# Earlier first loads in the attention head, and two low halves and an affine step moved in the pooling stage, of a two-block transformer kernel

## The reference, cut to what matters

```python
# layer 0, the head of the kernel
sh1, sc1, g1, sh2, sc2, g2 = split(silu(c) @ w_mod[0] + b_mod[0])    # w_mod: 1024 x 6144
hx = x * (1 + sc1) + sh1           # latent tokens
hc = ctx * (1 + csc1) + csh1       # 256 context tokens
q = rope(hx @ w_qkv[:, :1024]); k, v from hx and hc with the other columns
...
# layer 1, the pooling stage, between the first feed-forward and the second
x  = layer_norm(ALPHA * x + g2 * (hidden @ ffn_w_out[0]))
hx = x * (1 + sc1) + sh1
pooled = window means of hx (windows 2, 4, 8, 16) - hx
x  = layer_norm(ALPHA * x + g1 * ((pooled @ w_pool) * pool_scale))
h  = (x * (1 + sc2) + sh2) @ ffn_w_in[1] ...
```

## Time and profile before

| | |
|---|---|
| median of three runs | 1114.23 us (1114.17 to 1116.12) |
| profiled execution | 1114.73 us |
| its span, first to last instruction | 1113.0 us |
| PE busy | 1099.3 us, 99% of the span |
| DVE busy | 776.3 us, 70% |
| ACT busy | 587.0 us, 53% |
| chain of work that ended last | PE 92%, DVE 3%, DMA 3%, ACT 1% |

### The profile page before, as it was taken

How to read it: one execution, slowest core, us unless ns; L and a number is a source line. 1 busy time by engine, 2 the same in 40 slices (tenths; PEclk the granted TensorE clock), 3 DMA queues, 4 the chain that set the end, 5 groups by cost and what they waited for, 6 DMA issues and landing times.

```text
span 1113.0 us, 14486 instructions
## 1 busy us (share of the span) xinstructions
PE 1099.3 (99%) x5851; PEld 910.0 (82%) x5851; DVE 776.3 (70%) x1007; ACT 587.0 (53%) x821; POOL 61.4 (6%) x118
## 2 busy tenths in 40 slices
PE   8999999999999999999999999999999999999998
PEld 4688766899998887888887878878888888888886
DVE  2596588889889797877745865455566677774454
ACT  3742376563454347555534767556754466563342
POOL 0011200002121001000000000000000000000000
PEclk9999999999999999999999999999999999999999
DMA  9987740679999946667567788786524455555541
GB/s 363 403 309 249 243 163 1 208 255 349 379 383 332 350 146 232 224 211 269 183 199 126 223 177 190 155 180 134 177 76 152 152 196 203 207 189 189 189 161 38
DMA packets 111986, 238.31 MB, mean 214 GB/s; under 512 B 5712, under 2 KB 51920, under 8 KB 110640
## 3 DMA queue, kind: packets, MB, share of 16 engines
q1 hardware_dynamic: 97280, 185.42, 53.2%
q0 software_dynamic: 14352, 51.72, 13.1%
q10 hardware_dynamic: 288, 0.26, 0.1%
HBM read 236.29 MB, written 1.07 MB: 213 GB/s over the span
## 4 chain that ended last, share of the span: by engine, by line
PE 92%; DVE 3%; DMA 3%; ACT 1%; issue 0%; SPq 0%; ACTq 0%
PE ps L2068 19%; PE ps L2069 19%; PE ps L2070 19%; PE ps L2136 10%; PE ps L2138 5%; PE ps L2105 4%; PE ps L2104 4%; PE ps L2103 4%; PE ps L2253 2%; DMA raw<-in_attn_w_qkv 2%; PE ps L2388 1%; PE ps L2356 1%; DMA raw<-in_qkv_first 1%; DVE wL L1213 1%; PE ps L2277 0%; PE ps L2621 0%
## 5 line engine op out<-in xcount | busy, mean ns | idle before, releaser
L1213 DVE TENSOR_TENSOR wL<-raw,wH 128x1024 fp32r<-128x1024 f32 x326 | 394.7, 1222 | 211.3 <-ACT wH L638 208.9
L638 ACT ACTIVATE wH<-raw 128x1024 fp32r<-128x1024 f32 x326 | 340.3, 1058 | 300.4 <-PE ps L2070 196.1
L2068 PE MATMUL ps<-wH,aHL 128*128 128x512 f32 x576 | 229.3, 398 | 2.4 <-DVE aHL L1616 0.9
L2069 PE MATMUL ps<-wL,aHL 128*128 128x512 f32 (+1 forms) x592 | 229.0, 387 | 0.0
L2070 PE MATMUL ps<-wH,aHL 128*128 128x512 f32 x576 | 224.8, 390 | 0.0
L2136 PE MATMUL ps<-aHL,wH 128*128 128x512 f32 x480 | 168.8, 397 | 0.0
L2068 PEld LDWEIGHTS ps<-wH,aHL 128*128 128x128 f32 x576 | 108.1, 188 | 35.1 <-issue 7.1
L2138 PE MATMUL ps<-aHL,wL 128*128 128x256 f32 x480 | 134.1, 279 | 0.0
L2069 PEld LDWEIGHTS ps<-wL,aHL 128*128 128x128 f32 x592 | 111.3, 188 | 20.8
L2070 PEld LDWEIGHTS ps<-wH,aHL 128*128 128x128 f32 x576 | 108.1, 188 | 23.4
L2136 PEld LDWEIGHTS ps<-aHL,wH 128*128 128x128 f32 x480 | 90.1, 188 | 21.7
(11 more groups left out here) (330 smaller groups left out, 1491.7 us busy)
## 6 DMA issues: line engine op xcount, KB each, us to landing
raw<-in_ffn_w_in SPq DMA_DIRECT2D x88, 512.0 KB
modraw<-in_mod_rows POOLq DMA_DIRECT2D x80, 512.0 KB, 6.6
raw<-in_w_in SPq DMA_DIRECT2D x32, 1024.0 KB
raw<-in_ffn_w_out SPq DMA_DIRECT2D x22, 1024.0 KB
raw<-in_w_up SPq DMA_DIRECT2D x16, 1024.0 KB
raw<-in_w_down SPq DMA_DIRECT2D x16, 1024.0 KB
mod<-in_mod_first SPq DMA_DIRECT2D x8, 1024.0 KB, 16.8
raw<-in_attn_w_qkv SPq DMA_DIRECT2D x8, 1024.0 KB
```

The costliest lines, as they stand in the source:

```text
L638: nc.scalar.activation(wHigh(n), raw[:, (n // 2) % RAW, (n % 2) * 1024:(n % 2) * 1024 + 1024], ACT.Copy).then_inc(w_hi, 1)
L1213: V.tensor_tensor(wL[:, n % WL, :], raw[:, (n // 2) % RAW, (n % 2) * 1024:(n % 2) * 1024 + 1024], wHigh(n).bitcast(fp32), ALU.subtract).th ...
L2068: T.matmul(outp, xh, h, start=first, stop=False, skip_group_check=part_of)
L2069: T.matmul(outp, xh, l, start=False, stop=False, skip_group_check=part_of)
```

## The change

In the head: each half of `mod0` and the first half of each query weight get a semaphore of their own. ACT's `adv` of an even sub below 8 waits for the first half only. The load of `cb` moves behind sub 11, the loads of `cst`'s second part and `x` behind sub 15, and ACT's `silu` of `cb` from group 2 to the place behind `adv(16)`. PE does `mod_mm(0)` without waiting for `cst`, has fewer filler calls (5 to 3, 4 to 3, and 1 to 0), and takes `mod_mm(s + 1)` one part earlier. ACT and DVE take `adv(6)` ahead of `mod_copy(3)` and `mod_put(3)`. The tiles `cols` and `vcol` are widened from 113 to 128 and from 80 to 96 columns.

In the pooling stage: `adv(first + 2)` and `adv(first + 3)` on DVE move into `residual(0)` and `residual(1)`, behind the first half of each. `affine(1)` moves ahead of `adv(first + 4)`.

```diff
-        cols = sb(ctx, "cols", [P, 113])
+        cols = sb(ctx, "cols", [P, P])
-        vcol = sb(sA, "vcol", [P, len(VECS) * KT])
+        vcol = sb(sA, "vcol", [P, 96])
-        mod0_in = [sem(f"mod0_in{i}") for i in range(NMOD0)]
+        mod0_in = [sem(f"mod0_in{i}") for i in range(2 * NMOD0)]
+        q_first = [sem(f"q_first{i}") for i in range(4)]
 # SP
             for m in range(NMOD0):
                 for h in range(2):
-                    ... .then_inc(mod0_in[m], 16)
+                    ... .then_inc(mod0_in[2 * m + h], 16)
-                for c in range(2):
-                    sp.dma_start(raw[:, m, c * D:(c + 1) * D], a["qkv_first"][:, m, c, :]).then_inc(w_raw[m], 16)
-                if m == 1:
-                    sp.dma_start(cb[:, :], a["c"].to_broadcast([P, D])).then_inc(cb_in, 16)
+                sp.dma_start(raw[:, m, 0:D], a["qkv_first"][:, m, 0, :]).then_inc(q_first[m], 16)
+                sp.dma_start(raw[:, m, D:2 * D], a["qkv_first"][:, m, 1, :]).then_inc(w_raw[m], 32)
             for c in range(2, 6):
                 chunk(SUBS["qkv"] + 4 * c, a["attn_w_qkv"][0], c * CW)
                 if c == 2:
+                    sp.dma_start(cb[:, :], a["c"].to_broadcast([P, D])).then_inc(cb_in, 16)
+                elif c == 3:
                     sp.dma_start(cst[:, C_DIST:C_END], ...)
                     sp.dma_start(x[:, :, :], ...)
 # ACT
-                if n % 2 == 0:
+                if n < 8 and n % 2 == 0:
+                    act.wait_ge(q_first[n // 2], 16)
+                elif n < 8 or n % 2 == 0:
                     act.wait_ge(w_raw[(n // 2) % RAW], 32 * (n // WL + 1))
             for c in range(NMOD0):
+                if c == 3:
+                    adv(2 * c)
                 if c:
                     act.wait_ge(mod_sel, c)
                 mod_copy(c)
-                adv(2 * c)
+                if c < 3:
+                    adv(2 * c)
                 act.wait_ge(mod_out, c + 1)
                 hi_x(c, *mc(c))
                 adv(2 * c + 1)
-                if c == 2:
-                    act.wait_ge(cb_in, 16)
-                    nc.scalar.activation(cb[:, :], cb[:, :], ACT.Silu).then_inc(cb_ready, 1)
             for c in range(2, 6):
                 for j in range(3):
                     adv(n + 4 * c + WS + j)
+                    if (c, j) == (2, 0):
+                        act.wait_ge(cb_in, 16)
+                        nc.scalar.activation(cb[:, :], cb[:, :], ACT.Silu).then_inc(cb_ready, 1)
                     if (c, j) == (2, 1):
                         heads_out(0)
 # DVE, head
             for c in range(NMOD0):
+                if c == 3:
+                    adv(2 * c)
                 mod_put(c)
-                adv(2 * c)
+                if c < 3:
+                    adv(2 * c)
 # DVE, ln_pool
                 def residual(t):
                     for b in range(2):
                         ...
                         V.bn_stats(...).then_inc(dve_self, 1)
                         links[0] += 1
+                        if b == 0:
+                            adv(first + 2 + t)
                 for j in range(2):
                     low(j)
-                adv(first + 2)
                 for j in range(2, 4):
                     low(j)
                 ...
                 hat(0, halves[1], ln_hat)
-                adv(first + 3)
+                dve.wait_ge(pool_h, TT + 1)
+                affine(1)
                 adv(first + 4)
                 low_x3(0, 0, 0)
                 adv(first + 5)
                 low_x3(0, 0, 1)
-                dve.wait_ge(pool_h, TT + 1)
-                affine(1)
                 scaled(1)
 # PE
-                pe.wait_ge(mod0_in[c], 32)
                 for h in range(2):
+                    pe.wait_ge(mod0_in[2 * c + h], 16)
-            zero_mm(5, 4)
-            pe.wait_ge(cst_in, 16)
+            zero_mm(3, 4)
             pe.wait_ge(cT_ready, 2)
             mod_mm(0)
+            pe.wait_ge(cst_in, 16)
             mod_select(0)
-            zero_mm(4, 5)
+            zero_mm(3, 5)
             for s in (1, 2):
                 q_mm(0, s)
+                mod_mm(s + 1)
                 q_mm(1, s, range(1))
-                mod_mm(s + 1)
-                q_mm(1, s, range(1, 2))
                 mod_select(s + 1)
-                q_mm(1, s, range(2, 4))
-                if s == 1:
-                    zero_mm(1, 5)
+                q_mm(1, s, range(1, 4))
```

More of the change, by code:

```diff
@@ L467, in _ @@
                 for h in range(2):
-                    sp.dma_start(mod0[:, 2 * m + h, :], a["mod_first"][:, m, h, :]).then_inc(mod0_in[m], 16)
+                    sp.dma_start(mod0[:, 2 * m + h, :], a["mod_first"][:, m, h, :]).then_inc(mod0_in[2 * m + h], 16)
                 sp.dma_start(xT[:, 2 * m:2 * m + 2, :], a["x_cols"][:, 2 * m:2 * m + 2, :]).then_inc(x_in[m], 16)
-                for c in range(2):
-                    sp.dma_start(raw[:, m, c * D:(c + 1) * D], a["qkv_first"][:, m, c, :]).then_inc(w_raw[m], 16)
-                if m == 1:
-                    sp.dma_start(cb[:, :], a["c"].to_broadcast([P, D])).then_inc(cb_in, 16)
+                sp.dma_start(raw[:, m, 0:D], a["qkv_first"][:, m, 0, :]).then_inc(q_first[m], 16)
+                sp.dma_start(raw[:, m, D:2 * D], a["qkv_first"][:, m, 1, :]).then_inc(w_raw[m], 32)
             sp.dma_start(ctxT, a["ctx_cols"]).then_inc(ctx_in, 16)
@@ L690, in mod_copy @@
                 nc.scalar.activation(modrow[:, :], ps[:, 6, :], ACT.Copy).then_inc(mod_row, 1)
-            act.dma_start(cols[:, :], a["cols"]).then_inc(cols_in, 16)
+            act.dma_start(cols[:, 0:113], a["cols"]).then_inc(cols_in, 16)
             act.dma_start(cst[:, 0:C_DIST], cst_d[:, 0:C_DIST]).then_inc(cst_in, 16)
```

## The result

The changed kernel takes **1106.71 us** (median of four runs, 1105.58 to 1107.98) where the kernel before took 1114.90 beside it (1114.17 to 1116.12). The ratio is 0.9926, with a 95% interval of 0.9909 to 0.9943: 8.2 us, or 0.7%, faster. The forecast was 1114.3, and its range ended at 1111.6.

What follows compares the result with a forecast made beforehand. PE, busy 99% of the span, was taken as the bound, with one load setting the head and DVE's queue the pooling stage. Head +1.0 and pooling -0.9 on 1114.23 gave 1114.3 us, range 1111.6 to 1116.8.

Steps and rivals of the forecast that it cites:

- item 7: Head, widened tiles: the shift of tiles behind them gets no price; bound 0 to 1.0 us of landing time.
- two events that the prediction named as proof against it: Head: the landing of subs 16 and 17 moves by more than a microsecond, or the clock falls.
- item 4: Head, ACT: adv(6) waits for its load, mod_copy(3) cannot start before 38.6, holding mod_select(3) for about 1 us.
- Item 1: Head, first loads with own signals: PE's first query product starts 1.2 to 1.3 us sooner, near 15.2.
- item 5: Head: the load of subs 16 and 17 lands at 65.4 as before, so nothing is left of PE's 1.5 us lead.
- Item 6: Head, ACT: silu of cb between adv(16) and adv(17) costs +1.0 us; heads(1) moves to 69.05, PE's wait becomes 3.1.
- rival B: Head: the clock falls in the 3.1 us wait before heads(1), costing 1.8 us, giving 1116.1; chance 0.27.
- The estimate of 1.6 us in the prediction: Head loads: by the skill's 256-byte descriptor rule, landing would come 1.6 us earlier; not counted in the sum.
- The steps behind: Pooling stage: pooled(1) and its chain come 1.0 us sooner, and PE wins 1.6 us from later waits.
- the one in front: Pooling stage: residual(1) ends about 0.8 us late, so PE waits +0.7 us for hm before the second window products.
- Rival D: Pooling stage: the 0.7 us delay stays since the waits behind are ACT's, giving 1115.9; chance 0.15.
- C: Head: the load of subs 16 and 17 is not the bound and lands sooner, giving 1110.8 to 1111.8; chance 0.15.

Runs made afterwards that it cites:

- a1: The kernel before with only the two tiles cols and vcol widened; 1106.59 us, ratio 0.9923.
- a3: The head's part of the change alone on the kernel before, narrow tiles, pooling stage as before; 1116.16 us, ratio 1.0018.
- a2: The changed kernel with the narrow tiles, so the whole change without the widening; 1115.16 us, ratio 1.0003.
- a4: The kernel before with the pooling stage's part of the change alone, narrow tiles; 1113.79 us, ratio 0.9988.
- g1: The changed kernel with the silu of cb moved ahead of adv(16) on ACT; 1105.90 us, ratio 0.9921.
- c1: The changed kernel with every tile 32 bytes later, weights too, so all at 160; 1108.87 us, ratio 0.9941.
- c2: The changed kernel with a 128-byte gap behind lrw: tiles behind it at 256, weights and aHL at 128; 1114.64 us, ratio 0.9990.
- c3: The changed kernel with a 256-byte gap behind lrw: tiles behind it at 384, weights and aHL at 128; 1108.48 us, ratio 0.9942.
- b2: The changed kernel with gaps that move wH from 128 to 160 and, unintended, hH to 256; 1114.84 us, ratio 0.9996.
- b3: The changed kernel with gaps that move aHL from 128 to 160 and, unintended, hH and uH to 256; 1118.07 us, ratio 1.0023.

## Why the prediction was wrong

**The step that failed is item 7 of the head: "Instructions get no price, as no row shows one that depends on this."** A row did. The page and the groups of before hold `aHL` at 390 ns and `hH` and `uH` at 395, in products of one shape, one line and one weight tile. I had worked out that the widening moves the tiles behind it, and then looked only at loads for an effect. The grouped rows of PE would have asked the question: what do `hH` and `uH` have in common that `aHL` has not? The size follows from counts, as an estimate. 528 matmuls with `hH` or `hL` at 6.9 ns less per step and 384 with `uH` or `uL` at 6.6 give 3.6 + 2.5 us. 96 with `cH` or `cL` and 96 with `oa`, taken at 6.6 too, give 1.3. That is 7.4 us where item 7 had nothing. a1 measured 8.6 (7.1 to 9.9), so 1.2 us (-0.3 to 2.5) of it is not accounted for; the row of line 2136 under a1 shows that profiled executions differ by more than that for another, unknown reason.

Neither of the two events that the prediction named as proof against it came up where it looked for them. The load kept its time, and in the changed kernel's profile the granted clock is 1.00 from 66 to 80 us. Both watch the head, and nothing in the list of signs watched the pace of a matmul.

**Head, items 1 to 6.** The path was right and the figures near. `adv(6)` stands ahead of `mod_copy(3)` and waits for its load; timeline of ACT in the changed kernel:

```profile
38.31 1.06 ACT L641 ACTIVATE wH<-raw 128x1024 fp32r<-128x1024 f32 x1 [1.75 <-DMA raw<-in_qkv_first]
40.23 0.60 ACT L693 ACTIVATE modrow<-ps 128x512 f32<-128x512 f32 x1 [0.86 <-PE ps L2286]
```

The adv was forecast at 37.6 to 38.6 and ran from 38.31 to 39.37. But the copy behind it then waited 0.86 us for PE, so it was not `adv(6)` that held it in this execution, in which PE was late for the reason below. In a3, where PE was not late, the copy follows `adv(6)` at once, at 38.78 (38.6 forecast), as item 4 has it; timeline of ACT:

```profile
38.78 0.58 ACT L693 ACTIVATE modrow<-ps 128x512 f32<-128x512 f32 x1
```

Item 1 forecast the first query product at 15.2. In a3 it started at 15.26, but in the changed kernel's profiled execution at 16.98, later than before. Timelines of PE, a3 and then the changed kernel, and the changed kernel's windows from 5 to 17 us:

```profile
11.80 2.82 PE L2303 MATMUL ps<-g1b 128*128 128x512 f32 x6
15.26 0.47 PE L2077 MATMUL ps<-wH,aHL 128*128 128x512 f32 x1 [0.63 <-DVE aHL L1321]
```

```profile
12.50 5.47 PE L2303 MATMUL ps<-g1b 128*128 128x512 f32 x6
16.98 1.42 PE L2077 MATMUL ps<-wH,aHL 128*128 128x512 f32 x1
```
```profile
5.00:12.00 7.00, 3.98 (x25) 1.35 (x23) 0.00 (x0) 0.91 (x3) 0.00 (x0) 0.97 1.01 375
12.00:17.00 5.00, 5.00 (x10) 2.42 (x10) 2.74 (x6) 3.82 (x6) 0.00 (x0) 0.50 1.01 425
```

The six fillers took 5.47 us for 2.82, at a granted clock of 0.50 (the 1.2 GHz level) over the whole window; in the 7 us ahead of it PE had been busy for 3.98. This cost nothing at the end, as item 5 has it: PE's work ahead of `heads(1)` is slack, and the wait became 1.5 us (3.1 forecast). In a3, with the full clock there, it is 3.09, as forecast. Item 6 had `heads(1)` at 69.05: 68.88 in the changed kernel, 68.87 in a3, 68.98 in a2. The head was forecast at +1.0; a3 measured +2.0, with an interval from +1.0 to +3.0, and +1.2 by the medians. So the forecast stands at the lower end of what was measured. What may stand on top is rival B, whose clock drop some executions show; its share in a3's runs was not shown.

**Loads.** The load of subs 16 and 17 landed 0.12 us sooner than before, inside item 7's bound of 0 to 1.0. The estimate of 1.6 us in the prediction was misapplied. The Trainium skill (DMA: Bandwidth & Descriptors, How a descriptor splits into AXI transactions) counts starts from multiples of 256 bytes, and the shifted tiles start 128 bytes past one: they are off it after the change as they were before. So that rule promised nothing here, and the landing does not test it.

**Pooling stage.** The steps behind hold, the one in front does not. In a4, which has this part alone, PE lost 0.1 us in front for the +0.7 forecast; the 0.76 us in the changed kernel comes with the faster products. Of the waits of 0.89 and 0.37 us behind the earlier trace rows, one of 0.4 us is left; waits of PE on others in the changed kernel, 400 to 440 us:

```profile
PE ps L2077 <- DVE aHL L1627: 0.4, 1, 0.4
```

Forecast -0.9; a4 measured -1.3 (-2.3 to -0.3), so by its time alone the forecast stands, with its step in front priced too high. Rival D fell.

**Rivals.** C fell: the load kept its time. B was half right: the clock does fall in or behind this wait in some executions, even in g1 with a wait of 2.0 us. The sum of everything but the widths was forecast at +0.1 and measured at +0.3 (-0.7 to +1.3) in a2. That the sum is so close is partly luck, as the head cost more than forecast and the pooling stage less. The error of the whole is item 7.

## What to carry to other kernels

Group the matmuls of a PE-bound kernel by form and operands, and ask about every pair of groups with one shape and two durations: 7 ns in a step of 237 were worth more than any edit to the order of the queues here. When a diff resizes any tile, work out where everything behind it now starts, and price instructions as well as loads. When tiles of a float32 product can be placed freely, start the stationary and the moving one at the same offset within 256 bytes, and measure it in the kernel at hand.

## What the runs showed of the hardware that was not expected

- **The pace of a float32 matmul depends on where its two SBUF tiles start relative to each other.** Records of 389 to 391 ns against 391 to 395, and about 7 ns less from start to start, for a stationary tile of 128 x 128 and 512 moving columns. Only the distance was seen to matter: c1 at 160 and 160 is fast, c2 at 128 and 256 is slow, c3 at 128 and 384 is fast. Why 256 bytes, no run here shows. The Trainium skill (SBUF — State Buffer, Operand start alignment) asks that an operand start at a multiple of its element size, and says of its own measurements that "these runs timed nothing". All starts here keep that rule, and the pace still differs.
- **With the operands the other way about, the sign may turn.** Where `aHL` moves and the weights are stationary (256 columns, line 2113 of the changed kernel), the mean was 283 ns with both at 128. In b2 (160 and 256) it was 281 and in b3 (128 and 160) 279. Changed kernel:

```profile
L2113 PE MATMUL ps<-aHL,wH 128*128 128x256 f32 x288 | 81.5, 283 | 0.0
```

  It is less than 1.2 us over 288 matmuls, and it is no rule. In line 2147 of the changed kernel, where `aHL` moves over the low weights, b3 has 282 ns for its 279, the other way about, and a1 has 277 with the changed kernel's layout. None of this is explained.
- **The granted clock fell in or behind a wait of 2 to 3 us between dense stretches in some executions and not in others of nearly the same program.** g1 had 0.65 from 69 to 71 us around a wait of 2.00, c1 0.50 from 71 to 74 behind one of 2.96; a2 had 1.00 all through after 3.28.
